# Final RMSNorm moved beside the last expert's products, with the turn-backs of every expert placed earlier

## What is computed

```python
def expert_choice_ffn(hn, w_router, w_gate, w_up, w_down):
    ...
    gate, idx = lax.top_k(aff.T, cap)
    xe = xt[idx]
    hdn = jax.nn.silu(jnp.einsum('ecd,edf->ecf', xe, w_gate)) * jnp.einsum('ecd,edf->ecf', xe, w_up)
    ye = jnp.einsum('ecf,efd->ecd', hdn, w_down) * gate[..., None].astype(hn.dtype)
    y = jnp.zeros_like(xt).at[idx.reshape(-1)].add(ye.reshape(-1, d))
...
x = x + expert_choice_ffn(rmsnorm(x, norm_ffn[l]), ...)
return rmsnorm(x, norm_final)
```

## Time and profile before

| | us |
|---|---|
| median of 3 runs | 2689.59 |
| lowest and highest run | 2687.23, 2692.03 |
| time of the profiled execution | 2687.12 |
| its span in the trace | 2685.2 |

### The profile page before, as it was taken

The page is one execution under the profiler, slowest core; times in us unless marked ns, Lnnn a source line. Parts: engine busy times, 40 slices in busy tenths (PEclk is TensorE's granted clock), DMA queues, the critical chain, the costliest instruction groups (busy, mean ns, idle before and its releaser), DMA issues. The chain is left out here.

```text
span 2685.2 us, 48640 instructions
## 1 busy us (share of the span) xinstructions
PE 2332.9 (87%) x20450; PEld 2088.7 (78%) x20450; DVE 1354.2 (50%) x1673; ACT 1076.2 (40%) x1584; POOL 380.5 (14%) x375
## 2 busy tenths in 40 slices
PE   3988899789999678698875999839999999999992
PEld 2766788789999667598772555439999999999992
DVE  4455411134545166233225443367777777777772
ACT  3555511011111056211115553226666666666662
POOL 0000000000000073344334121000000100100000
PEclk8999999899999878799997999869999999999996
DMA  3233421338666476454635441347877877777754
GB/s 112 55 84 98 118 97 72 111 102 269 182 199 190 122 224 211 107 154 111 208 78 192 140 133 64 134 155 268 275 254 261 273 264 262 269 261 265 265 162 174
DMA packets 182665, 468.24 MB, mean 174 GB/s; under 512 B 62800, under 2 KB 110576, under 8 KB 154688
## 3 DMA queue, kind: packets, MB, share of 16 engines
q1 hardware_dynamic: 169120, 417.65, 47.5%
q0 software_dynamic: 13344, 47.67, 6.3%
HBM read 366.91 MB, written 102.26 MB: 175 GB/s over the span
## 5 line engine op out<-in xcount | busy, mean ns | idle before, releaser
L77 DVE TENSOR_TENSOR ex_w_rest<-weights,ex_w_rounded 128x2048 fp32r<-128x2048 f32 x192 | 439.3, 2289 | 208.4 <-ACT ex_w_rounded L2224 206.6
L2224 ACT CAST ex_w_rounded<-weights 128x2048 fp32r<-128x2048 f32 x192 | 366.6, 1911 | 30.3 <-PEq L47 30.3
L84 PE MATMUL tk_acc<-tk_w_rounded,normed 128*128 128x336 f32 x800 | 257.9, 322 | 19.2 <-DVE tk_w_rest L77 19.2
L2118 PE MATMUL ex_g_acc<-ex_xt,ex_w_rounded 128*128 128x320 f32 x1024 | 271.3, 349 | 1.4 <-issue 1.4
L2118 PE MATMUL ex_u_acc<-ex_xt,ex_w_rounded 128*128 128x320 f32 x1024 | 271.0, 349 | 0.0
L84 PE MATMUL tk_acc<-tk_w_rounded,normed_rest 128*128 128x336 f32 x800 | 255.4, 319 | 0.0
L84 PE MATMUL tk_acc<-tk_w_rest,normed 128*128 128x336 f32 x800 | 255.2, 319 | 0.0
L2119 PE MATMUL ex_g_acc<-ex_xt,ex_w_rest 128*128 128x160 f32 x1024 | 242.3, 237 | 0.0
L2119 PE MATMUL ex_u_acc<-ex_xt,ex_w_rest 128*128 128x160 f32 x1024 | 241.6, 236 | 0.0
L2119 PEld LDWEIGHTS ex_g_acc<-ex_xt,ex_w_rest 128*128 128x128 f32 x1024 | 196.9, 192 | 0.0
L2119 PEld LDWEIGHTS ex_u_acc<-ex_xt,ex_w_rest 128*128 128x128 f32 x1024 | 195.9, 191 | 0.0
(11 more groups left out here) (292 smaller groups left out, 5111.5 us busy)
## 6 DMA issues: line engine op xcount, KB each, us to landing
weights<-in_w_expert SPq DMA_DIRECT2D x192, 1024.0 KB, 5.6
proj_tok<-tk_stage SPq DMA_DIRECT2D x10, 1680.0 KB, 7.9
laq<-sc_laq SPq DMA_DIRECT2D x20, 768.0 KB, 4.1
dl_la<-laq SPq DMA_DIRECT2D x20, 768.0 KB, 4.6
tk_w<-in_w_tok SPq DMA_DIRECT2D x10, 1344.0 KB, 6.6
ch_w<-in_w_ch SPq DMA_DIRECT2D x24, 512.0 KB, 4.1
sc_rows<-rows SPq DMA_DIRECT2D x40, 256.0 KB, 6.3
sc_qk<-qkv_ch SPq DMA_DIRECT2D x40, 256.0 KB, 6.7
```

The lines of the kernel that those rows point to most:

```text
L77: return dve.tensor_tensor(out, whole, rounded.bitcast(F32), ALU.subtract)
L84: mm = pe.matmul(out, stationary[a], moving[b], start=(first and n == 0), stop=(last and n == len(pairs) - 1))
L2118: pe.matmul(bank[:, 0:2 * SLOTS], hi[:, cols], x.rearrange("p a n -> p (a n)"), start=first, stop=False, skip_group_check=True)
L2224: act.copy(w_hi[:, i % SPLIT], held[:, i % HELD]).then_inc(w_rounded, 1)
```

## The change

It has three parts.

1. In every expert e from 1 on, `turn_back(e-1, 0)` and `turn_back(e-1, 1)` on TensorE move from after pieces 2 and 4 to after pieces 1 and 2. On ScalarE and VectorE, `y_out(e-1, 0)` and `y_out(e-1, 1)` move from steps 3 and 5 to steps 2 and 3, still at the end of the step.
2. The final norm of all rows is done inside the expert phase. When the scatters of experts 0 to 14 are in and five slots of the weight ring are free, SP loads `x2` into these slots in five DMAs of 1 MB. ScalarE's squares and roots and VectorE's scaling go in pairs of tiles, beginning in step 9 of expert 15, and SP stores each tile.
3. Expert 15 no longer adds to `x2`. POOL gathers its 160 rows of `x2` as they are before it, VectorE adds the gated results, the rows are normed apart, and POOL scatters them to `y` after all ten plain tiles have been stored. `phase_final`, with its block and barrier, goes.

```diff
+LAST_E = EXPERTS - 1
+FINAL_SLOTS = NT // 2
...
+        fgain = xp
+        xall = held[:, 0:FINAL_SLOTS].rearrange("p s k c -> p (s k c)").rearrange("p (t c) -> p t c", c=D)
...
+                sp.wait_ge(xp_turned, 2 * GANGS)
+                sp.dma_start(fgain[:], io["norm_final"].partition_broadcast(P)).then_inc(fn_gain_in, 16)
+                sp.wait_ge(scattered, 32 * LAST_E)
+                sp.wait_ge(w_split, NP * EXPERTS - HELD + FINAL_SLOTS)
+                for h in range(FINAL_SLOTS):
+                    sp.dma_start(xall[:, 2 * h:2 * h + 2, :], dr["x2"][2 * h * P:2 * (h + 1) * P].rearrange("(t p) c -> p t c", p=P)).then_inc(fn_loaded[h], 16)
+                for t in range(NT):
+                    sp.wait_ge(fn_scaled, t + 1)
+                    sp.dma_start(y[t * P:(t + 1) * P, :], xall[:, t, :]).then_inc(fn_stored, 16)
+                sp.wait_ge(fn_stored, 16 * NT)
...
-                scatter(EXPERTS - 1)
-                pool.wait_ge(scattered, 32 * EXPERTS)
+                pool.wait_ge(scattered, 32 * LAST_E)
+                for (rows, buf, _), ix in zip(LAST_ROWS, (sample_idx, prompt_idx)):
+                    pool.indirect_dma_start(out=buf[:], out_offset=None, in_=dr["x2"], in_offset=bass.IndirectOffsetOnAxis(ap=ix[:, LAST_E:], axis=0)).then_inc(base_gathered, 16)
+                pool.wait_ge(fn_stored, 16 * NT)
+                for n, ((rows, buf, _), ix) in enumerate(zip(LAST_ROWS, (sample_idx, prompt_idx))):
+                    pool.wait_ge(rows_scaled, n + 1)
+                    pool.indirect_dma_start(out=y, out_offset=bass.IndirectOffsetOnAxis(ap=ix[:, LAST_E:], axis=0), in_=buf[:], in_offset=None).then_inc(rows_stored, 16)
+                pool.wait_ge(rows_stored, 32)
...
-                    if n:
+                    if n and e == LAST_E:
+                        pe.wait_ge(rows_added, 1)
+                    elif n:
                         pe.wait_ge(ys_act, 2 * e + 1)
                         pe.wait_ge(ys_dve, 2 * e + 1)
...
                         multiply(e, n)
+                        if n == 1 and e >= 1:
+                            turn_back(e - 1, 0)
                         if n == 2 and e >= 1:
-                            turn_back(e - 1, 0)
-                        if n == 4 and e >= 1:
                             turn_back(e - 1, 1)
...
+                def final_square(t):
+                    if t == 0:
+                        act.wait_ge(w_split, NP * EXPERTS - HELD + FINAL_SLOTS + 2)
+                    else:
+                        act.wait_ge(fn_sumsq, t)
+                    act.wait_ge(fn_loaded[t // H], 16)
+                    act.activation(squares, xall[:, t, :], ACT.Square, accum_out=ss[:, 0, t:t + 1]).then_inc(fn_sumsq, 1)
...
+                        if n == 2 and e >= 1:
+                            y_out(e - 1, 0)
                         if n == 3 and e >= 1:
-                            y_out(e - 1, 0)
-                        if n == 5 and e >= 1:
                             y_out(e - 1, 1)
...
+                        if e == LAST_E and n >= 9:
+                            final_square(2 * (n - 9))
+                            if n >= 10:
+                                final_root(n - 10)
+                            final_square(2 * (n - 9) + 1)
+                down_half(LAST_E, 3)
+                for pair in range(3, FINAL_SLOTS):
+                    final_square(2 * pair)
+                    final_root(pair - 1)
+                    final_square(2 * pair + 1)
+                final_root(FINAL_SLOTS - 1)
...
+                def add_rows(n):
+                    rows, buf, gain = LAST_ROWS[n]
+                    dve.wait_ge(y_turned, 2 * LAST_E + n + 1)
+                    dve.wait_ge(base_gathered, 32)
+                    for half in range(2):
...
+                        if e == LAST_E and n == 10:
+                            final_inverse(0)
+                        if e == LAST_E and n == 11:
+                            final_inverse(1)
+                            final_scale(0)
+                y_columns(LAST_E, 3)
+                final_inverse(2)
+                final_scale(1)
+                add_rows(0)
+                final_inverse(3)
+                final_scale(2)
+                add_rows(1)
+                final_inverse(4)
+                final_scale(3)
+                final_scale(4)
+                for n in range(2):
+                    scale_rows(n)
```

More of the change, by code:

```diff
@@ L1999, with phase_experts @@
 AHEAD = 3
-def phase_experts(nc, io, dr, ident, held, w_loaded):
+LAST_E = EXPERTS - 1
+FINAL_SLOTS = NT // 2
+def phase_experts(nc, io, dr, ident, held, w_loaded, y):
     with ExitStack() as ctx:
@@ L2030, in phase_experts @@
         yp = sb("ex_yp", [CAP_P, D])
+        fgain = xp
+        xall = held[:, 0:FINAL_SLOTS].rearrange("p s k c -> p (s k c)").rearrange("p (t c) -> p t c", c=D)
+        squares = held[:, FINAL_SLOTS].rearrange("p k c -> p (k c)")[:, 0:D]
+        squares_last = held[:, FINAL_SLOTS + 1].rearrange("p k c -> p (k c)")[:, 0:D]
+        ss = sb("fn_ss", [P, 3, NT + 2])
         g_acc = ps("ex_g_acc", [P, 2, 512])
@@ L2051, in phase_experts @@
         ys_act, ys_dve = sem("ex_ys_act"), sem("ex_ys_dve")
+        fn_loaded = [sem(f"fn_loaded{h}") for h in range(FINAL_SLOTS)]
+        fn_gain_in = sem("fn_gain_in")
+        fn_sumsq, fn_mean, fn_inverse, fn_rstd = sem("fn_sumsq"), sem("fn_mean"), sem("fn_inverse"), sem("fn_rstd")
+        fn_scaled, fn_stored = sem("fn_scaled"), sem("fn_stored")
+        base_gathered = sem("fn_base_gathered")
+        rows_added, rows_squared, rows_mean, rows_inverse, rows_rstd, rows_scaled = (sem(f"fn_rows_{n}") for n in ("added", "squared", "mean", "inverse", "rstd", "scaled"))
+        rows_stored = sem("fn_rows_stored")
+        H = NT // FINAL_SLOTS
+        LAST_ROWS = ((CAP_S, ys, gain_s), (CAP_P, yp, gain_p))
         def opens(e):
@@ L2284, in y_out, with final_root @@
                     act.activation(dst[:, 0:HALF], turned[0:rows, 0, :], ACT.Copy, scale=gain[:, e:e + 1]).then_inc(ys_act, 1)
+                def final_square(t):
[5 more added lines that the diff above has]
+                    act.activation(squares, xall[:, t, :], ACT.Square, accum_out=ss[:, 0, t:t + 1]).then_inc(fn_sumsq, 1)
+                def final_root(h):
+                    act.wait_ge(fn_inverse, h + 1)
+                    act.activation(ss[:, 2, H * h:H * h + H], ss[:, 1, H * h:H * h + H], ACT.Sqrt).then_inc(fn_rstd, 1)
                 for i in range(AHEAD):
@@ L2315, in _ @@
                             round_prompt(e // GANG + 1)
-                down_half(EXPERTS - 1, 3)
-                y_out(EXPERTS - 1, 0)
-                y_out(EXPERTS - 1, 1)
+                        if e == LAST_E and n >= 9:
[9 more added lines that the diff above has]
+                final_root(FINAL_SLOTS - 1)
+                for n, (rows, buf, _) in enumerate(LAST_ROWS):
+                    act.wait_ge(rows_added, n + 1)
+                    if n:
+                        act.wait_ge(rows_squared, n)
+                    act.activation(squares_last[0:rows], buf[:], ACT.Square, accum_out=ss[0:rows, 0, NT + n:NT + n + 1]).then_inc(rows_squared, 1)
+                    act.wait_ge(rows_inverse, n + 1)
+                    act.activation(ss[0:rows, 2, NT + n:NT + n + 1], ss[0:rows, 1, NT + n:NT + n + 1], ACT.Sqrt).then_inc(rows_rstd, 1)
             @block.vector
@@ L2404, in _ @@
                             rest_prompt(e // GANG + 1)
[L2405 to L2458, removed]
@@ L2482, in layer @@
             phase_merge(nc, io, dr, ident, mixer, mixer_ready, load_expert)
-            phase_experts(nc, io, dr, ident, held, w_loaded)
-        phase_final(nc, io, dr, y)
+            phase_experts(nc, io, dr, ident, held, w_loaded, y)
 def constants():
```

23 lines of the change are left out of this document (added).

## The result

The changed kernel takes 2706.48 us (median of 4 runs, 2705.09 to 2710.28) against 2689.59 before. The ratio is 1.0065 with a 95% interval of 1.0048 to 1.0082: slower, by 16.9 us between the medians. The forecast was 2711.7 with a range of 2700 to 2731. The profiled execution took 2706.74 us, its span is 2704.7 (2685.2 before).

The account below looks back on a forecast made before the run. The prediction took PE's own work to bound the expert phase and a chain of small steps the last 50 us; +39.0 + 4.3 - 21.2 = +22.1 us gave 2711.7 us, range 2700 to 2731.

Parts of the forecast that it names:

- Stall: Expert phase, experts 1 to 15: PE waits 2.60 us at the second turn-back for VectorE's y_out(e-1, 0), +39.0 us.
- none of the 2.60 if `y_out` slipped ahead: Lower bound of PE's wait per expert: none if VectorE's order let y_out go earlier; upper bound 2.65 us.
- Clock: Expert phase: PE's clock falls behind 2 in 11 of the 15 gaps, at 1.56 us each, +4.3 us.
- the clock holds: Rival: PE resumes at full rate after each gap in the expert phase; 2707.4 us, chance 0.20.
- Tail: After the last product: the final phase goes, scatters start 13.5 us later, 5.3 us follow the landing; saving -21.2 us.
- outer end of -25.7: Larger saving after the last product, if only 0.85 us and not 5.3 follow the last scatter's landing.
- the ending: Time from the last scatter's landing to the end: 0.85 to 5.3 us, taken as 5.3 since that row follows POOL's scatter.
- Loads of x at nothing: Expert 15: SP's loads of x cost nothing, covered by the idle DMA share; if late, they hold only ACT's squares.
- the forecast's own range: 2703 to 2722 us, from the short ending (-4.4), clock falls (-4.3 to about +8) and half a microsecond in the adds.

Follow-up runs that it names:

- the third experiment: The changed kernel with one line moved: VectorE does y_out(e-1, 0) in step 2 before it splits the weight piece; 2662.42 us, ratio 0.9901.

## Why the prediction was right, and which terms were mis-sized

The forecast came true for its own reasons, with sizes that missed on both sides and partly cancelled: clock +1.7, short pieces -2.0, tail -3.9. The sign, the place and the price of the stall are shown: it goes when one copy moves, it appears on the kernel before when only the moves are made, and it grows and shrinks by 0.4 us with the copy's place. Terms in the order of the sum:

- **Stall**, 15 x 2.60 = 39.0: measured 39.0. It was read without a run from where PE arrives and where VectorE's next free slot is. The bound "none of the 2.60 if `y_out` slipped ahead" is what the third experiment built.
- **Clock**, +4.3 from 2 falls in 11 gaps: 6.0 in the profiled execution. The step that failed in size was the share: 27 of 75 such gaps fell in five profiles, not 2 in 11, for about 9 us on average at 1.7 each. The 11 gaps of one execution were too small a sample: in the twelve profiles the same 11 gaps fell 1 to 5 times, 34 of 132 in all. They were also a mixture. A stall of 2.60 us has an idle time of 2.35 in the view, which is that of the three shorter gaps of the channel phase (2 of 3 fell in the profile before), not of the eight of 3.0 us and more (0 of 8). The rival "the clock holds" was excluded by every profile with gaps. The Trainium skill, "TensorE: Matmul & The Clock Gate", section "Why this matters for your kernels", warns only of longer gaps. The traces do not bear that out: the clock fell to 1.2 GHz behind gaps of 2.2 and 2.6 us.
- **The short pieces**, not in the sum: -2.0 us. This is what remains of the stretch's +43.0 once stall and clock are taken off. Most pieces take either 4.11 or 4.16 us, in stretches. Between first and last turn-back 107 pieces of the changed kernel take 4.11, 44 take 4.16 and 3 take 4.21; before, these were 82, 75 and 15. The transposes and matmuls are the same. What picks the pace was not found.
- **Tail**, -21.2 with an outer end of -25.7: measured -25.1. The parts from VectorE's last `ex_yt` were foreseen as 20.5 to the second scatter's start, 5.1 of landing and 5.3 of ending, 30.9 in all; they were 18.6, 2.8 and 5.6, so 27.0. VectorE's chain was 1.0 us shorter, in part since an inverse took 0.3 and not 0.4 (the adds took 0.70 a half, near the 0.74 assumed). POOL started 0.2 us after its release and not 0.7, its first scatter took 1.3 with its gap and not 1.85, and the write without an add landed in 2.8 us where that with an add had taken 5.1. The choice of 5.3 over 0.85 for the ending was right, for the reason given: POOL. So the tail came near the outer end of -25.7, but not by the short ending for which that end stood.
- **Loads of x at nothing**: the five were issued at 2653, and the first square started at 2665.24 directly behind ScalarE's copy. Nobody waited for them. The stores and VectorE's last row group were done together, at about 2694.8, as foreseen.

The sum of the sizes as measured is 39.0 + 6.0 - 2.0 - 25.1 = 17.9 in the profile, against 22.1 foreseen. The medians give 16.9. One slip in the working had no weight: the terms named for the forecast's own range reach up to about 2720 (2711.7 + 8 + 0.5), not 2722.

## What to carry to other kernels

When a hand-off is moved earlier on a busy engine, look up the slot at which the partner can answer, not only whether its work is small: a copy of 0.74 us behind 2.7 us of other work cost 2.6 us each time, 15 times, and in the partner's idle gap it cost nothing. Judge the parts of a change apart: here one part gave 25 us and the other took 43, and a single line turned +17 into -25. And where an engine that issues indirect DMAs ends last, try letting another engine hold the wait for them: here it gave 2.1 us, in the profiles of two kernels.

## What the runs showed of the hardware that was not expected

- Behind POOL's last step at the end of the block 5.5 to 5.6 us pass, whether that step is a wait, a memset or the issue of a scatter. Some 4.5 us of them are POOL's DRAIN, which took 0.03 us in a block where POOL had no work. With this time beside the landing, the 8.4 us from the last scatter's start to the end became 6.3.
- An indirect write to DRAM of 32 rows lands 2.8 us after its start; with an add, the last one of a kernel took 5.0 to 5.1.
- The granted clock falls to 0.50 behind some of a row of like gaps and not behind others, 3 to 8 of 15 from one execution to the next at 2.6 us; a fall costs 1.3 to 2.9 us. Once it fell behind a wait of only 1.7 us (at 2413.2 in the third experiment's profile), one of the 36 waits for `ex_xpt` between experts in the twelve profiles.
- A piece of 32 matmuls takes 4.11 or 4.16 us in one and the same profile; what picks one of the two was not looked into.
